# Block transposes on VectorE in place of TensorE transposes: x and the pooling input weights of a two-layer hybrid decoder trunk

## What is computed

```python
# layer 0: gated linear attention
h = x @ gla_w_in                      # [2048,1024] @ [1024,3088] -> q, k, v, g, lr
...
x = layernorm(ALPHA * x + mix(h) @ gla_w_out)
# layer 1: causal pooling mixer
u, z = split(x @ pool_w_in)           # [1024, 4096], u and z 2048 wide each
p = pooled(u, windows 2, 4, 8, 16) - u
m = einsum('btgc,gcd->btgd', p, pool_w_grp) + b_grp      # four groups of 512 x 512
y = (m * scale * silu(z)) @ pool_w_out
x = layernorm(ALPHA * x + y)
```

## Time and profile before

| | us |
|---|---|
| median of 3 runs | 1877.38 (1876.57 to 1878.32) |
| the profiled execution | 1877.09 |
| its span, first to last instruction | 1875.3 |
| PE (TensorE matmul) busy | 1834.0 (98%) |
| DVE (VectorE) busy | 1376.8 (73%) |
| ACT (ScalarE) busy | 842.1 (45%) |
| POOL (GpSimd) busy | 663.3 (35%) |

### The profile page before, as it was taken

One profiled execution on the slowest core, in us unless ns is written; L12 is line 12 of the kernel. 1 busy time (PEld: TensorE's weight loads), 2 busy tenths in 40 slices (PEclk: granted clock), 3 DMA queues, 4 the chain that ended last, 5 costly groups with the idle time before them and its releaser, 6 DMA issues.

```text
span 1875.3 us, 24024 instructions
## 1 busy us (share of the span) xinstructions
PE 1834.0 (98%) x8498; PEld 1503.2 (80%) x8498; DVE 1376.8 (73%) x1661; ACT 842.1 (45%) x1294; POOL 663.3 (35%) x460
## 2 busy tenths in 40 slices
PE   9999999999999899999989999999999999999997
PEld 8878886887788788888678888878888887887885
DVE  3566565768576888877786778678899978447997
ACT  4554335656646533444544444354444344224221
POOL 0433222322231000344435655315576533223330
PEclk9999999999999999999999999999999999999999
DMA  9967664449364945675724444243455436637442
GB/s 305 319 220 246 217 209 170 125 98 288 89 147 122 327 142 187 214 239 188 278 90 152 154 135 157 77 157 124 157 204 189 166 120 223 244 135 270 179 146 101
DMA packets 278243, 342.81 MB, mean 183 GB/s; under 512 B 48368, under 2 KB 206832, under 8 KB 273520
## 3 DMA queue, kind: packets, MB, share of 16 engines
q1 hardware_dynamic: 275440, 333.98, 54.0%
q0 software_dynamic: 2688, 7.34, 1.2%
HBM read 221.73 MB, written 119.54 MB: 182 GB/s over the span
## 4 chain that ended last, share of the span: by engine, by line
PE 83%; DVE 5%; issue 3%; ACT 1%; DMA 1%; POOL 1%; DVEq 0%; ACTq 0%; POOLq 0%
PE banks L224 25%; PE banks L226 25%; PE banks L225 25%; PE banks L1846 1%; PE banks L1850 1%; PE banks L975 1%; DVE m_w_lo L2867 1%; DVE m_x_lo L2881 1%; PE banks L2650 1%; PE banks L948 1%; DMA m_ahead<-x_terms 1%; DVE a_w_lo L2117 0%; PE banks L1624 0%; PE banks L1007 0%; PE banks L2610 0%
## 5 line engine op out<-in xcount | busy, mean ns | idle before, releaser
L224 PE MATMUL banks<-m_x_hi,m_w_hi 128*128 128x512 f32 x1312 | 514.6, 392 | 10.5 <-DVE m_z L2942 4.4
L226 PE MATMUL banks<-m_x_hi,m_w_lo 128*128 128x512 f32 x1312 | 513.0, 391 | 0.0
L225 PE MATMUL banks<-m_x_lo,m_w_hi 128*128 128x512 f32 x1312 | 512.5, 391 | 0.0
L224 PEld LDWEIGHTS banks<-m_x_hi,m_w_hi 128*128 128x128 f32 x1312 | 246.7, 188 | 67.4 <-DVE m_w_lo L2867 7.8
L225 PEld LDWEIGHTS banks<-m_x_lo,m_w_hi 128*128 128x128 f32 x1312 | 246.7, 188 | 53.4 <-issue 0.7
L226 PEld LDWEIGHTS banks<-m_x_hi,m_w_lo 128*128 128x128 f32 x1312 | 246.6, 188 | 52.2
L224 PE MATMUL banks<-b_hi,h_w_hi 128*128 128x512 f32 x656 | 257.4, 392 | 4.0 <-issue 3.5
L225 PE MATMUL banks<-b_lo,h_w_hi 128*128 128x512 f32 x656 | 256.1, 390 | 0.0
L226 PE MATMUL banks<-b_hi,h_w_lo 128*128 128x512 f32 x656 | 256.1, 390 | 0.0
L2674 ACT ACTIVATE m_w_hi<-m_s 128x512 fp32r<-128x512 f32 x182 | 114.4, 629 | 204.3 <-PE banks L226 174.8
L2867 DVE TENSOR_TENSOR m_w_lo<-m_s,m_w_hi 128x512 fp32r<-128x512 f32 x182 | 163.4, 902 | 33.1 <-ACT m_w_hi L2674 32.0
(11 more groups left out here) (279 smaller groups left out, 3354.7 us busy)
## 6 DMA issues: line engine op xcount, KB each, us to landing
b_raw<-x_in SPq DMA_DIRECT2D x14, 1024.0 KB, 9.6
m_x_raw<-x_terms SPq DMA_DIRECT2D x9, 1024.0 KB, 8.0
p_in<-in_pool_w_in SPq DMA_DIRECT2D x32, 256.0 KB, 5.5
w_fused<-p_out SPq DMA_DIRECT2D x32, 256.0 KB, 3.9
x_in<-h_terms SPq DMA_DIRECT2D x8, 1024.0 KB, 4.3
v_tiles<-h_v_out SPq DMA_DIRECT2D x16, 512.0 KB, 5.0
in_raw<-in_gla_w_in SPq DMA_DIRECT2D x16, 512.0 KB, 5.4
h_raw<-in_gla_w_in SPq DMA_DIRECT2D x16, 512.0 KB, 5.4
```

The costliest lines, as they stand in the source:

```text
L224: nc.tensor.matmul(out, a_hi, b_hi, start=first, stop=False, skip_group_check=True)
L225: nc.tensor.matmul(out, a_hi, b_lo, start=False, stop=False, skip_group_check=True)
L226: return nc.tensor.matmul(out, a_lo, b_hi, start=False, stop=last, skip_group_check=True)
```

## The change

TensorE turns neither x nor the pooling input weights any more. VectorE turns them in 32x32 squares. Such an instruction moves nothing between groups of 32 partitions, so the loads put the right block of rows and columns on each group: four DMAs of 32 partitions where there was one of 128. The contraction index then lies in another order (channel g*256 + k*32 + j on partition g*32 + j), so the grouped and the projection weights are loaded in the same order, also by DMAs of 32 partitions. x is turned straight into the operand buffers of `project`; it is still stored to `x_in`, for steps 8 to 23, but in steps 0 to 7 not read back. Of the 16 x tiles two are turned in `prepare`, two at the start of `project`, and two in each of steps 0 to 5 (VectorE, at n = 1 and 3). TensorE's `turn` and `turn_x`, their calls, and ScalarE's copies of turned x are gone from both functions; the nine warm-up matmuls at the start stand together. The first group's weights are loaded from ScalarE's queue. `load_pair` is left for steps 8 to 23.

```diff
+    def load_x_rows(self, sp, u):
+        t = self.x_tile(u)
+        src = self.a["x"][0][t * P:(t + 1) * P, :].rearrange("(b i) c -> i b c", i=SQUARE)
+        for g in range(QUADS):
+            sp.dma_start(self.x_rows[u % 2][g * SQUARE:(g + 1) * SQUARE, :].rearrange("i (b c) -> i b c", b=QUADS),
+                         src[:, :, g * D // QUADS:(g + 1) * D // QUADS]).then_inc(self.x_rows_loaded[u % 2], DMA)
+    def turn_x(self, dve, u, raw):
+        dve.wait_ge(self.x_rows_loaded[u % 2], (u // 2 + 1) * QUADS * DMA)
+        out = raw[:, u % 2 * KT:(u % 2 + 1) * KT, :].rearrange("p k (b i) -> p b k i", i=SQUARE)
+        self.nc.vector.transpose(out, self.x_rows[u % 2][:].rearrange("p (b k j) -> p b k j", b=QUADS, j=SQUARE)
+                                 ).then_inc(self.x_turned, 1)
+    def store_x(self, sp, u, raw):
+        sp.wait_ge(self.x_turned, u + 1)
...
+    def by_rows(self, w):
+        return w.rearrange("(g k j) c -> g j k c", g=QUADS, j=SQUARE)
 def prepare(nc, p, a):
-    PAIR_AT = 23
+    TURNS_AT = {16: 0, 17: 1}
+    ROWS_AT = {9: 0, 10: 1, 18: 2, 19: 3}
...
+    t_raw = [p.place(f"p_t_raw{s}", [P, GT, P]) for s in range(2)]
...
                 def load_in(n):
                     if n >= IN:
                         sp.wait_ge(turned, n - IN + 1)
-                    sp.dma_start(w_in[n % IN][:], src_in[n % KT, :, n // KT * GW:(n // KT + 1) * GW]
-                                 ).then_inc(in_loaded[n % IN], DMA)
+                    for q in range(QUADS):
+                        first = n // KT * GW + q * P
+                        sp.dma_start(w_in[n % IN][q * SQUARE:(q + 1) * SQUARE, :].rearrange("i (b c) -> i b c", c=P),
+                                     src_in[n % KT, :, :, first:first + P]).then_inc(in_loaded[n % IN], DMA)
...
                 def load_values(j, n):
                     k, c = V_LOADS[j]
-                    sp.dma_start(p.b_raw[j][:, n, :], v_src[:, k + n, 2 * KD + c:2 * KD + c + BLK]
+                    sp.dma_start(p.b_raw[j][n * SQUARE:(n + 1) * SQUARE, :, :],
+                                 v_src[n, :, k:k + HALF_K, 2 * KD + c:2 * KD + c + BLK]
                                  ).then_inc(b_loaded[j], DMA)
                 def load_grp(g):
-                    for c in range(GT):
-                        if g:
-                            sp.wait_ge(g_lo, (g - 1) * GT + c + 1)
-                        sp.dma_start(w_grp[:, c, :], src_grp[:, g, c, :]).then_inc(grp_loaded[c], DMA)
+                    sp.wait_ge(g_lo, g * GT)
+                    for q in range(QUADS):
+                        sp.dma_start(w_grp[q * SQUARE:(q + 1) * SQUARE, :, :], src_grp[g, q]).then_inc(grp_loaded, DMA)
...
-                load_in(0)
-                load_grp(0)
-                for n in range(1, IN - 1):
+                for n in range(IN - 1):
                     load_in(n)
-                load_x(0)
...
+                for q in range(QUADS):
+                    act.dma_start(w_grp[q * SQUARE:(q + 1) * SQUARE, :, :], src_grp[0, q]).then_inc(grp_loaded, DMA)
-                    nc.scalar.activation(t_hi[n % 2][:].rearrange("p c d -> p (c d)"), turned_ps[n % 2],
-                                         ACT.Copy).then_inc(hi, 1)
+                    nc.scalar.activation(t_hi[n % 2][:], t_raw[n % 2][:], ACT.Copy).then_inc(hi, 1)
-                        nc.scalar.activation(x_out[t % 2][:], x_ps[t % 2], ACT.Copy).then_inc(x_copied, 1)
...
+                def turn(n):
+                    dve.wait_ge(in_loaded[n % IN], (n // IN + 1) * QUADS * DMA)
+                    nc.vector.transpose(t_raw[n % 2][:].rearrange("p t (b i) -> p b t i", i=SQUARE),
+                                        w_in[n % IN][:].rearrange("p (b t j) -> p b t j", b=QUADS, j=SQUARE)
+                                        ).then_inc(turned, 1)
+                for n in range(2):
+                    turn(n)
                 for n in range(TILES):
                     dve.wait_ge(hi, n + 1)
...
+                    if n + 2 < TILES:
+                        dve.wait_ge(lo, n + 1)
+                        turn(n + 2)
                     if n == 0:
                         for c in range(GT):
                             grp_part(0, c)
...
+                    if n in TURNS_AT:
+                        p.turn_x(dve, TURNS_AT[n], p.in_raw0)
 def project(nc, p, a, phase, last_copy, last_store, ahead):
+    X_AT = (1, 3)
...
             for b in range(2):
-                sp.dma_start(raws[i % 2][:, b * KT:(b + 1) * KT, :], w_src[:, :, column(i, b):column(i, b) + P]
-                             ).then_inc(pair_loaded[i % 2], DMA)
+                for g in range(QUADS):
+                    sp.dma_start(raws[i % 2][g * SQUARE:(g + 1) * SQUARE, b * KT:(b + 1) * KT, :],
+                                 w_src[g, :, :, column(i, b):column(i, b) + P]).then_inc(pair_loaded[i % 2], DMA)
...
-                if n == 0 and i + 2 < STEPS:
+                if n == 0 and V_STEPS <= i + 2 < STEPS:
...
+                if i + 2 < V_STEPS and n in X_AT:
+                    u = 2 * (i + 2) + X_AT.index(n)
+                    p.store_x(sp, u, raws[i % 2])
+                    if u + 2 < NT:
+                        p.load_x_rows(sp, u + 2)
...
+                if n in X_AT and i + 2 < V_STEPS:
+                    turn_x(i + 2, X_AT.index(n))
```

More of the change, by code:

```diff
@@ L145, in __init__ @@
         assert self.at <= SBUF_END
+        self.at = self.rows_at + 2 * D * 4
+        self.x_rows = [self.place(f"x_rows{b}", [P, D]) for b in range(2)]
         self.mix_raw_at = self.rows_at - 2 * KT * P * 4
@@ L247, in prepare @@
     out = [p.place(f"p_out{s}", [P, GW]) for s in range(2)]
-    x_out = [p.place(f"p_x{s}", [P, KT, P]) for s in range(2)]
-    rows = [p.place(f"p_rows{s}", [P, D]) for s in range(ROWS)]
+    t_hi = [p.place(f"p_t_hi{s}", [P, GT, P], F32R) for s in range(2)]
+    t_lo = [p.place(f"p_t_lo{s}", [P, GT, P], F32R) for s in range(2)]
+    t_raw = [p.place(f"p_t_raw{s}", [P, GT, P]) for s in range(2)]
+    p.at = p.in_end + 9 * KT * P * 4
     grp_hi, grp_lo = [], []
@@ L253, in prepare @@
         grp_lo.append(p.place(f"p_grp_lo{s}", [P, GT, GW], F32R))
-    t_hi = [p.place(f"p_t_hi{s}", [P, GT, P], F32R) for s in range(2)]
-    t_lo = [p.place(f"p_t_lo{s}", [P, GT, P], F32R) for s in range(2)]
-    assert p.at <= SBUF_END
+    assert p.at <= p.w_end
     with ExitStack():
@@ L463, in _ @@
                             pe.wait_ge(g_lo, g * GT + c + 1)
-                        if n == 0 and c == 2:
-                            turn(1)
                         last = split_product(nc, out_ps[n % 2], t_hi[n % 2][:, c, :], t_lo[n % 2][:, c, :],
@@ L615, in project @@
     terms = p.place("h_terms", [P, 4, BLK])
-    p.at = g_at
-    rows = p.place("h_rows", [P, D])
-    x_out = p.place("h_x_out", [P, KT, P])
     p.at = p.qkv_end
@@ L999, in turn_keys @@
                 last.then_inc(turned, 1)
-        def turn_x(u):
-            pe.wait_ge(rows_loaded, (u - KT + 1) * DMA)
-            if u > KT:
-                pe.wait_ge(x_copied, u - KT)
-            for k in range(KT):
-                last = nc.tensor.transpose(p.ps[:, 6 + k // HALF_K, k % HALF_K * P:(k % HALF_K + 1) * P],
-                                           rows[:, k * P:(k + 1) * P], p.ident[:])
-            last.then_inc(x_turned, 1)
         for i in range(STEPS):
@@ L1443, in norm_of, with turn_x @@
                                         ALU.mult).then_inc(normed, 1)
-        for n in range(PREPARED, PRODUCTS):
+        def turn_x(i, b):
+            o = i - 2
+            if o >= 0:
+                dve.wait_ge(w_hi_done, PRODUCTS * (o + 1))
+                dve.wait_ge(w_lo_done, parts_to(o, PRODUCTS - 1))
+                dve.wait_ge(x_summed, 4 * (o + 1))
+                dve.wait_ge(p.x_stored, 2 * (o + 1) * DMA)
+                if o:
+                    dve.wait_ge(w_summed, 4 * o)
+            p.turn_x(dve, 2 * i + b, raws[i % 2])
+        turn_x(1, 0)
+        for n in range(PREPARED, HALF_K):
+            lo_part(0, n)
+        turn_x(1, 1)
+        for n in range(HALF_K, PRODUCTS):
             lo_part(0, n)
```

168 lines of the change are left out of this document (44 added, 124 removed).

## The result

The change makes the kernel slower. The median of the changed kernel is 1891.26 us (1890.0 to 1892.24), of the kernel before 1877.22 in the same session: a ratio of 1.0073, 95% interval 1.0060 to 1.0086, some 14 us. The forecast of 1868.0 is 23 us off and the result lies outside its range; the rival with slow loads gave 1896.

The account below looks back on a forecast made before the run. TensorE, busy 98% of the span, was taken as the bound, with SP's queue setting the pace in prepare's middle. Gains of 7.1 in project and 2.3 in prepare, 9.4 us, gave 1868.0 us; range 1858 to 1879.

Parts of the forecast that it names:

- the rival with slow loads: DMA queue in prepare: loads to 32 partitions move at half rate, stage end at 146, time 1896; chance 0.11.
- the price of the DMA engines' work in `prepare`: prepare up to iteration 19: 70 us of DMA work, from 3 to 73, at 286 and 364 GB/s by piece length.
- SP's 85: prepare, middle: SP's queue sets the pace and stores tile 18 at 85 us.
- the argument against full queues: prepare: the change takes bytes out, 28 instead of 35 MB, said against SP being held up by full queues.
- its signs: Half rate in prepare would show as tile-load landings over 8 us at DMA share 1 with fewer GB/s.
- SP's queue: prepare: short issues at 0.50 us each, 2.0 us a tile, with nearly no waits in 20 to 85 us.
- the rival of full queues: prepare: SP's issues take 0.60 us each, 10.4 us more, time 1878, no change; chance 0.14.
- The start: Start of prepare: first product near 11.7 instead of 7.64, 4 us lost, bounds 0 to 6.
- Steps 0 to 7: project: VectorE's turns, 1.4 us each, are hidden and the full 7.1 us of removed transposes is gained.
- Steps 8 to 23: project: eight pair-load issues instead of two, 3 us more a step on SP, hidden; taken as 0, bounds 0 and +1.3 twice.
- The sum: Whole kernel: 7.1 from project plus 2.3 from prepare, 9.4 us gained.

Follow-up runs that it names:

- experiment 4: Changed kernel with prepare's loads of tiles, w_grp, b_raw and x rows in 128 partitions instead of 32, as many loads: 1880.64 us, ratio 1.0015.
- experiment 2: Kernel of loads alone, 256 KB each in 2 KB pieces, by partitions covered: 357 GB/s over 128 partitions, 216 for one quarter alone, 237 over 64.
- experiment 6: Kernel with prepare's loads in 128 partitions and one load a tile (1872.62 us), pair loads of steps 8 to 23 also in 128: 1867.17 us, ratio 0.9937.

## Why the prediction was wrong

**The step that failed** is the price of the DMA engines' work in `prepare`: "512-byte pieces ran at 286 GB/s, 2 KB pieces at 364", taken from loads of 128 partitions, gave 70 us up to iteration 19, "close behind SP's 85, not ahead". The loads of 32 partitions don't run at those rates. The stage moved 241 and 245 GB/s at a share of 1.08, and 9.0 us of its length are theirs (experiment 4). An estimate: with the 226 GB/s of experiment 2 for tiles, v and groups and 231 for the rows of x, that same sum is 92 us in place of 70 and ends at 95, behind SP's 85. SP came to the store of tile 18 at 95.58; that it fits so well is partly luck, since with 128 partitions it still came at 89.36 and not 85. Fewer bytes, the argument against full queues, bought nothing: 28 MB at 243 in place of 330 GB/s are more work than 35.

**The rival had the mechanism and too high a price.** It was to decide "under some 250 GB/s" (by its own terms, 16.5 MB of loads in 82 - 19.4 us, already under 264), and 243 came. Its half of 364 was 182; alone the loads had 210 to 237, and in the stage stores of 128 partitions ran between them. It put the stage's end at 146 and the time at 1896; they were 134 and 1891. Of its signs the full engines with fewer GB/s came and landings over 8 us did not:

```profile
p_in<-in_pool_w_in SPq DMA_DIRECT2D x128, 64.0 KB, 4.3
```

(The row is the page's: four loads of one quarter to a tile, median us to landing.) Its chance of 0.11 was too low: the section of the Trainium skill that the prediction quotes ("SBUF — State Buffer", Door 1: The DMA port swizzle) said it, and no row spoke against it, since none had a full queue of such loads.

**SP's queue was priced a little low.** 0.5 us an issue and hardly a wait in 20 to 85 us: both came. From the end of the group loads to the store of tile 18 the working had 69.7 us (15.3 to 85). With 128 partitions they took 75.0 (14.4 to 89.36), with 32 78.7 (16.9 to 95.58). What it left out are waits, 4.7 of the 9.0 us too few with 32 partitions and 2.6 of the 5.3 with 128. The rest are issues that take longer, as in these two rows, changed kernel and 128 partitions:

```profile
58.97 1.36 SPq L349 DMA_DIRECT2D b_raw<-in_gla_w_in  x1
```

```profile
30.33 1.53 SPq L350 DMA_DIRECT2D b_raw<-in_gla_w_in  x1
```

That fits the rival of full queues, in part and on top of the other. From the store to the end of the stage the working had 33.2 us; it took 35.7 and 38.5. So the 9.0 us of the partitions lie in three places: 2.5 at the start, 3.7 in the middle, 2.8 in the tail. VectorE may have a part in the tail: the working gave it 2.9 us a tile, and with GpSimd at work beside it a low part took 1.74 in place of 0.69 us. Rows of VectorE, then the one of GpSimd, changed kernel:

```profile
91.34 0.69 DVE L501 TENSOR_TENSOR p_t_lo<-p_t_raw,p_t_hi 128x512 fp32r<-128x512 f32 x1
...
97.23 2.29 DVE L523 TENSOR_TENSOR b_lo<-b_raw,b_hi 128x1024 fp32r<-128x1024 f32 x1
99.44 1.74 DVE L501 TENSOR_TENSOR p_t_lo<-p_t_raw,p_t_hi 128x512 fp32r<-128x512 f32 x1
```

```profile
94.21 6.43 POOL L407 TENSOR_TENSOR b_raw<-b_raw,b_raw 128x512 f32<-128x512 f32 x4 [11.04 <-DMA b_raw<-in_gla_w_in]
```

This is new with the change. Before, the low part read its tile from PSUM (`banks` in the earlier trace rows) and none of the 32 took longer than 0.694 us, though GpSimd made the same sums; now both its inputs are in SBUF, the longest takes 1.775 us and all 32 take 27.8 us in place of 22.0. The working took over the old 0.69. What that costs the run was not tried.

**The start** was priced at 4 us, first product at 11.7. It came at 13.46, and at 10.97 with 128 partitions: 2.5 us of the start are the partitions again. TensorE had been idle for 7.75 us and ran its first matmul in 0.77 us, at a granted mean of 0.57 in 8 to 14 us, where the working had allowed up to 1.5 us for the clock.

**Steps 0 to 7** gave 5.7 of 7.1 us. The turns were cheaper than thought, 1.2 us for 1.4 (the group's row, changed kernel, busy and mean ns):

```profile
L189 DVE STREAM_TRANSPOSE in_raw<-x_rows 128x1024 f32<-128x1024 f32 x2 | 2.4, 1203 | 0.0
```

They were hidden but for one wait, 1.61 us at 153.01, for VectorE's `h_v_out`. That wait is as long as what is missing (1.4 us); that the turns cause it was not tried. In the two kernels with the x part alone the same stretch was 163.3 and 163.5 us, 3 us more than in the change; why stays open.

**Steps 8 to 23** were taken at 0, bounds 0 and +2.6, "since megabytes are already queued". It was +4.8, above the bound. At the first reload of x nothing was lost: TensorE waited 2.69 us before step 8, 2.93 before the change. The loss is behind the second one. TensorE before the change, then the changed kernel:

```profile
460.40 0.47 PE L224 MATMUL banks<-b_hi,h_w_hi 128*128 128x512 f32 x1 [0.54 <-issue]
```

```profile
466.41 0.47 PE L248 MATMUL banks<-b_hi,h_w_hi 128*128 128x512 f32 x1 [1.24 <-ACT banks L1022]
...
474.42 0.47 PE L248 MATMUL banks<-b_hi,h_w_hi 128*128 128x512 f32 x1 [1.34 <-DVE b_lo L1247]
```

With two more waits, 0.79 at 505.76 and 1.12 at 512.60, and one of 0.67 at 470.07 these make 5.2 us in 460 to 515 where there were 0.9. In the kernel of experiment 6, with the pairs in 128 partitions, 1.3 us are left there and its whole stretch is 5.0 us shorter. So the place was right and the size wrong: the bound counted SP's issues only. That the missing part is the lower rate at which the queued megabytes then move fits the later landings of x (10.9 us in place of 9.6); no run parts the two.

**Sum.** The sum was -9.4. The start and `prepare` give -2.3 in it and +13.6 in the trace, 15.9 apart, of which 9.0 are the partitions and 6.9 were still missing without them, 4.4 up to the store of tile 18 and 2.5 behind it; steps 0 to 7 are off by 1.4, steps 8 to 23 by 4.8.

## What to carry to other kernels

Before an exchange that saves an engine's work by loads over fewer partitions, price the loads at the rate of the new shape with full queues, and if no row of the trace has that, measure it alone first: a kernel of loads alone would have given the 222 GB/s, under the rival's threshold. Count both things that a load of 32 partitions costs, the rate (0.6 here) and the issues (four for one, 0.47 us each), and look where both already run full. A change in two halves is worth trying by halves: x, whose own loads are mostly in a stage with room (share 0.63 to 0.82 in 121 to 280 us of that kernel), gained 2.5 us; the pooling weights, with 12.6 MB of loads in a full stage, lost 19. And ask where the new instruction leaves its result: moved from PSUM to SBUF, it made the next one of VectorE slower beside GpSimd.

## What the runs showed of the hardware

A set of 32-partition loads costs no more DMA time than one of 128 partitions in equal pieces while the engines are half idle (136 and 138 GB/s, both at share 0.50), and 1.6 times as much when they are full (222 against 361 GB/s). Two quarters 32 partitions apart move no more than one (210 and 216), two from different halves 8 to 10% more (233 and 237). In the changed kernel the order 0, 2, 1, 3 in place of 0, 1, 2, 3 was worth 5 us of 1891, at no cost (ratio 1.0046 in place of 1.0073). A float32 low part of 128x512 with both inputs in SBUF took 0.69 us on VectorE alone and 1.74 beside GpSimd's sums; with one input in PSUM it took at most 0.694.
